# K pages of the paged cache kept in natural layout, turned in place in 32x32 blocks by VectorE and scored in 32-row, 32-column tiles of TensorE, 16 pages at a time

## Chip, cores and metric

One core of one Trainium2 chip runs the whole program once. The metric is the device time in microseconds. The kernel before took 1212.95 us (median of 3 runs, 1209.15 to 1214.07).

## What is computed

One layer of a hybrid decoder, for one prompt of 512 positions and for 8 samples of 8 new positions each, with the same weights. The part that the change touches is the attention of the samples to their paged cache: 32 pages of 128 keys per sample, 8 heads of 64.

```python
def sb_logits(q, k, sb_bias):
    z = jnp.einsum("bqhd,bkhd->bhqk", q, k).astype(jnp.float32) * SB_SCALE
    return z + sb_bias.astype(jnp.float32)[None, :, None, None]

def sb_block(z, mask, v, carry):
    log_om = jnp.where(mask, jax.nn.log_sigmoid(-z), 0.0)
    suffix = lax.cumsum(log_om, axis=3, reverse=True) - log_om + carry[..., None]
    a = jnp.where(mask, jnp.exp(jax.nn.log_sigmoid(z) + suffix), 0.0)
    o = jnp.einsum("bhqk,bkhd->bqhd", a, v.astype(jnp.float32))
    return o, carry + jnp.sum(log_om, axis=3)

    def page_step(state, phys):
        o_acc, carry = state
        kp = cache_k[phys]
        vp = cache_v[phys]
        zp = sb_logits(q, kp, sb_bias)
        o_p, carry = sb_block(zp, True, vp, carry)
        return (o_acc + o_p, carry), None
```

The pages of a sample are taken from the newest to the oldest, since each needs the product of the (1 - beta) of all newer keys. The rest of the layer is: the input projection (q, k, v and three convolution inputs), the same attention inside the prompt, a gated convolution, the output projection, cross attention to a memory of 256 tokens, and a SwiGLU of width 2816. All is float32. The large products are made of three passes over a high and a low part of each operand (`w_hi`, `w_lo`, `h_hi`, `h_lo`).

## The kernel before

Five in-order instruction streams (TensorE, VectorE, ScalarE, GpSimd, SyncE) are written out by hand and meet at semaphores. The program has a front of 32 **chunks** and, behind them, the output projection, cross attention and the SwiGLU. The samples are worked on in 4 groups of two; a group has 8 chunks, and a chunk has 4 pages of each of the two samples, 8 pages of 256 KB for K and as many for V. SyncE issues the K pages (`k_pages`, L610) and the weights, GpSimd issues the V pages (`v_pages`, L610) and makes the low parts of weights (`tile_lo`, L940).

What chunk C does, in the order of TensorE's stream (`group`, which calls the functions named here):

- `k_transposes(C + 1)` (L1651): 8 pages, 4 transposes of 128x128 each, through three PSUM banks. ScalarE copies the even pages out (`copy_k`, L1029) and VectorE the odd ones (`copy_k`, L1307), to `kT`, where the 64 dimensions of two heads lie on the 128 partitions.
- `tile(2C + 2)` (L1570): 128 columns of the input projection, in chunks 0 to 10; VectorE scales the result out of PSUM (`evac`, L1291, L1295). Of the 32 tiles, 24 belong to the prompt and sample projection and 8 to the memory (`mem_tile_chunk`).
- `weight_transposes` (L1687) for chunk C, then `prompt_transposes` (L1623) of an earlier unit of prompt attention.
- `scores(C + 1)` (L1676): 8 matmuls of 128 rows and 32 columns against 512 keys, four column tiles side by side.
- `tile(2C + 3)`, again in chunks 0 to 10; `prompt_scores(u)` (L1611, L1614), where u = C - LAST counts 16 units of prompt attention (4 head pairs by 4 query blocks, the number of key blocks is u mod 4 plus 1).
- `sums(C)` (L1708): the weights of 8 pages times V; `prompt_sums` (L1636).

ScalarE makes the two sigmoids of a chunk's scores (`sample_sigmoids`, L1035 and L1037) and of the prompt's (`prompt_sigmoids`, L1057), and copies weights out of PSUM. VectorE makes the suffix products with a scan and multiplies (`weights`, L1317, L1324, L1327 for the samples; `prompt_weights`, L1334, L1340 for the prompt), and copies half of the prompt's transposed weights (`copy_prompt_weights`, L1348). In VectorE's stream a chunk is: `evac`, `copy_k`, `evac`, in some chunks a piece of the convolution, `copy_prompt_weights`, `prompt_weights`, `weights`. At a group's end it copies the sums out (L1414), TensorE transposes them, and VectorE copies the result into place (L1419). `queries` (L1354) lays the next group's queries block-diagonally into `q_bd`.

The waits that set the order around the change are these lines. A page's slot is free when it has been transposed:

```python
if C:
    sp.wait_ge(s_ktr, 8 * C + q - 7)
```

and the scores of a chunk wait for both copying engines:

```python
pe.wait_ge(m_["k_copied_a"], 4 * C + 4)
pe.wait_ge(m_["k_copied_d"], 4 * C + 4)
```

V pages have 10 slots in the chunks before LAST and 12 after it.

## Time and profile before

| | before |
|---|---|
| runs | 1212.95 us median (1209.15 to 1214.07) |
| profiled execution, own time | 1204.37 us |
| its span, first to last instruction | 1202.7 us |
| granted TensorE clock, mean | 0.978 |
| TensorE busy | 1107.7 us (92%) |
| VectorE busy | 624.4 us (52%) |
| ScalarE busy | 397.0 us (33%) |
| GpSimd busy | 409.1 us (34%) |
| read from HBM | 213.78 MB |
| chain that ended last: TensorE, VectorE, DMA | 75%, 12%, 7% |

The busy shares are averages over stretches with different limits. The front ends at about 595 us; what follows is almost all dense matmul. A float32 matmul that is not split into high and low parts shows as two records in the trace, one per pass; a transpose shows as one. Where matmuls run side by side in tiles of the array, the busy time of a group is the time in which at least one of them ran, and its mean is that of one record, from start to drained end.

### The profile page before, as it was taken

The page shows a single profiled execution, that of the slowest core. Times are in us where ns is not written, and L with a number is a line of the kernel's source. Part 1 is how long each engine was busy: PE and PEld are TensorE (multiplying, and loading weights), DVE is VectorE, ACT ScalarE, POOL GpSimd, SP SyncE. Part 2 cuts the span into 40 slices and gives each one's busy share as a digit, 9 for nine tenths or more (in the row PEclk, how much of TensorE's full clock was granted, in tenths as well). Part 3 has the DMA queues.
Part 4 walks back from the last instruction along what each step waited for, and adds up shares of the span by engine and source line. Part 5 has one row for each costly group of instructions (what it writes and reads, how often), then busy time and mean ns, then how long its engine had stood idle before and what let it go on. Part 6 is the DMA issues. An engine that isn't in the chain of part 4 may idle for free.

```text
span 1202.7 us, 25986 instructions
## 1 busy us (share of the span) xinstructions
PE 1107.7 (92%) x9831; PEld 978.0 (81%) x9831; DVE 624.4 (52%) x854; ACT 397.0 (33%) x624; POOL 409.1 (34%) x341
## 2 busy tenths in 40 slices
PE   6799999899697999899699888899999999999997
PEld 3687888777465777667599858899999999999996
DVE  2645535644555776675588357655543002544544
ACT  3533323233453655453523162412111112112121
POOL 0425344432322443344342003333433333433330
PEclk9899999999988999999899999899999999999999
DMA  9858676855997889897752033222221223231212
GB/s 348 303 153 303 226 289 217 281 203 189 373 333 271 302 316 353 318 363 275 238 210 70 29 112 106 71 82 93 70 87 53 92 88 100 70 105 44 66 65 78
DMA packets 126489, 220.96 MB, mean 184 GB/s; under 512 B 9951, under 2 KB 68580, under 8 KB 126388
## 3 DMA queue, kind: packets, MB, share of 16 engines
q1 hardware_dynamic: 103234, 146.63, 35.5%
q0 software_dynamic: 20480, 67.13, 15.7%
q10 hardware_dynamic: 2674, 5.87, 1.4%
q8 instruction: 62, 1.02, 0.3%
q14 instruction: 39, 0.32, 0.1%
HBM read 213.78 MB, written 5.80 MB: 183 GB/s over the span
## 4 chain that ended last, share of the span: by engine, by line
PE 75%; DVE 12%; DMA 7%; issue 2%; ACT 2%; SPq 2%; POOLq 0%; POOL 0%; DVEq 0%; ACTq 0%
PE ps L513 38%; PE ps L1570 14%; PE ps L1651 8%; PE ps L1676 4%; DMA k_page<-in_cache_sb_k 3%; PE ps L1708 3%; PE ps L574 2%; DMA mw_raw<-in_w_in 2%; DVE r_sq L671 1%; DVE h_lo L418 1%; DVE r_sum L676 1%; DVE run L1334 1%; DMA v_late<-in_cache_sb_v 1%; DVE run_s L1317 1%; DVE aw L1340 1%
## 5 line engine op out<-in xcount | busy, mean ns | idle before, releaser
L469 POOL TENSOR_TENSOR w_lo<-w_raw,w_hi 128x2048 fp32r<-128x2048 f32 (+3 forms) x49 | 192.9, 3939 | 395.4 <-ACT w_hi L446 359.7
L513 PE MATMUL ps<-h_hi,w_hi 128*128 128x288 f32 x832 | 180.0, 298 | 8.7 <-DVE h_lo L418 5.7
L513 PE MATMUL ps<-h_lo,w_hi 128*128 128x288 f32 x832 | 179.2, 297 | 0.0
L513 PE MATMUL ps<-h_hi,w_lo 128*128 128x288 f32 x832 | 179.1, 297 | 0.0
L1651 PE MATMUL ps<-cc,k_page 128*128 128x128 f32 x1024 | 142.0, 290 | 36.5 <-DVE kT L1307 14.2
L1651 PEld LDWEIGHTS ps<-cc,k_page 128*128 128x128 f32 x1024 | 117.8, 148 | 59.5 <-issue 44.2
L446 ACT ACTIVATE w_hi<-w_raw 128x2048 fp32r<-128x2048 f32 (+3 forms) x47 | 77.9, 1660 | 255.1 <-PE ps L513 227.2
L610 POOL DMA_DIRECT2D v_late<-in_cache_sb_v x168 | 90.3, 537 | 171.5 <-issue 109.4
L513 PEld LDWEIGHTS ps<-h_hi,w_hi 128*128 128x128 f32 x832 | 135.2, 190 | 9.8 <-issue 7.2
L513 PEld LDWEIGHTS ps<-h_hi,w_lo 128*128 128x128 f32 x832 | 135.1, 190 | 0.0
L513 PEld LDWEIGHTS ps<-h_lo,w_hi 128*128 128x128 f32 x832 | 135.1, 190 | 0.0
L1307 DVE COPY kT<-ps 128x512 f32<-128x512 f32 x128 | 87.8, 691 | 90.4 <-PE ps L1651 90.1
L940 POOL TENSOR_TENSOR mw_lo<-mw_raw,mw_hi 128x1024 fp32r<-128x1024 f32 x32 | 78.9, 2466 | 109.3 <-ACT mw_hi L1010 109.2
L1029 ACT ACTIVATE kT<-ps 128x512 f32<-128x512 f32 x128 | 75.9, 597 | 105.4 <-PE ps L1651 105.1
L1570 PE MATMUL ps<-h_hi,mw_hi 128*128 128x288 f32 (+1 forms) x288 | 81.0, 336 | 2.9 <-DVE h_lo L418 2.8
L1570 PE MATMUL ps<-h_hi,mw_lo 128*128 128x288 f32 (+1 forms) x288 | 78.7, 328 | 0.0
L1570 PE MATMUL ps<-h_lo,mw_hi 128*128 128x288 f32 (+1 forms) x288 | 78.4, 327 | 0.0
L610 POOL DMA_DIRECT2D v_early<-in_cache_sb_v x88 | 47.6, 542 | 88.9 <-PE ps L1708 53.9
L513 PE MATMUL ps<-f_hi,w_hi 128*128 128x288 f32 x352 | 75.4, 296 | 0.0
L513 PE MATMUL ps<-f_lo,w_hi 128*128 128x288 f32 x352 | 75.4, 296 | 0.0
L513 PE MATMUL ps<-f_hi,w_lo 128*128 128x288 f32 x352 | 75.3, 296 | 0.0
L666 DVE TENSOR_TENSOR xT<-ps,xT 128x576 f32<-128x576 f32 (+1 forms) x32 | 24.2, 758 | 97.8 <-PE ps L513 97.2
(252 smaller groups left out, 1818.9 us busy)
## 6 DMA issues: line engine op xcount, KB each, us to landing
k_page<-in_cache_sb_k SPq DMA_DIRECT2D x256, 256.0 KB, 5.2
v_late<-in_cache_sb_v POOLq DMA_DIRECT2D x168, 256.0 KB, 5.2
v_early<-in_cache_sb_v POOLq DMA_DIRECT2D x88, 256.0 KB, 4.9
mw_raw<-in_w_in SPq DMA_DIRECT2D x12, 1024.0 KB, 5.2
w_raw<-in_w_gate SPq DMA_DIRECT2D x11, 1024.0 KB, 5.3
w_raw<-in_w_up SPq DMA_DIRECT2D x11, 1024.0 KB, 5.4
w_raw<-in_w_down SPq DMA_DIRECT2D x8, 768.0 KB, 4.2
w_raw<-in_w_down SPq DMA_DIRECT2D x8, 640.0 KB, 4.0
```

The source lines that it names most:

```text
L446: nc.scalar.activation(w_hi[s][:, 0:KN[name], :], w_raw[s][:, 0:KN[name], :], ACT.Copy).then_inc(s_whi, 1)
L469: return nc.gpsimd.tensor_tensor(w_lo[s][:, ks, :], w_raw[s][:, ks, :], w_hi[s][:, ks, :].bitcast(F32), ALU.subtract)
L513: op = nc.tensor.matmul(ps[:, 2 * t + hf, 0:b - a], weights[s][:, k, t * P:(t + 1) * P], x[:, k0 + k, a:b], start=begin and k == ks[0] and ...
L610: eng.dma_start(slot, cache[0, bass.ds(page, 1)].rearrange("o p h d -> p o (h d)")).then_inc(loaded, 16)
L666: nc.vector.tensor_tensor(x, pair(j % 2), x, ALU.add).then_inc(s_free[name], 1)
L940: nc.gpsimd.tensor_tensor(mw_lo[j // 2 % 2][:, :, t], mw_raw[j // 2 % 2][:, :, t], mw_hi[j % 2][:, :, :].bitcast(F32), ALU.subtract).then_ ...
L1029: nc.scalar.activation(kT[:, q // 4, :, (q % 4) * P:(q % 4 + 1) * P], tiled(ps[:, q % 3, :]), ACT.Copy).then_inc(m_["k_copied_a"], 1)
L1307: nc.vector.tensor_copy(kT[:, q // 4, :, (q % 4) * P:(q % 4 + 1) * P], tiled(ps[:, q % 3, :]))\
L1570: op = nc.tensor.matmul(ps[:, bank, 0:b - a], weights, x[:, k, a:b], start=k == 0 and w == 0, stop=k == KD - 1 and w == 2)
L1651: op = nc.tensor.transpose(ps[:, q % 3, j * P:(j + 1) * P], k_page[:, q, j * P:(j + 1) * P], ident)
L1676: op = nc.tensor.matmul(ps[32 * j:32 * j + 32, 3, :], q_bd[:, s, j, :], kT[:, s, j, :], start=s == 0, stop=s == 1)
L1708: op = nc.tensor.matmul(ps[32 * j:32 * j + 32, 6, s * P:(s + 1) * P], awT_s[C >= LAST][:, q, 32 * j:32 * j + 32], page[:, 0, j * P:(j + 1) ...
```

## The change

The four functions of the K path are replaced. Pages are loaded in **halves**: half H = 2U + s is 8 pages of one of the group's two samples (s), and the pair of halves U is 16 pages, as much as two chunks. There are two sets of 8 page slots (`k_set`), one per sample; SyncE may fill a set when the scores of the half that lay in it are made. VectorE turns two pages at a time in place, in 32x32 blocks (`k_blocks`, one instruction of 128x1024, four to a half). After that, partition group `a` (32 partitions) holds 32 dimensions of the keys 32a to 32a + 31, and TensorE scores a half with 64 matmuls of 32 rows, 32 columns and 256 keys (`half_scores`): 2 halves of the dimensions, 4 head pairs, 4 row groups that write PSUM banks 0 to 3, and 2 heads that take two of the four column groups. The queries are spread for this by `query_blocks` on TensorE (16 small matmuls a group) and by 24 small copies on VectorE in `queries`.

The sigmoids, scans and products are made for a pair of halves, at odd chunks: one sigmoid of 1024 columns (beta), and twice a sigmoid of 512 (1 - beta), a scan, a product and a copy of the carry (`page_sigmoids`, `page_weights`, parts 0 and 1). `om_s` is now scanned in place, so that the second sigmoid waits for the first scan and carry. At the head of an even chunk TensorE waits until the second sigmoid has read the score banks (`banks_read`), since its memory tiles and items use banks 1 to 3. The new positions' scores have rows of their own (`new_scores`, `new_sigmoids`, `new_weights`), at the seventh chunk of a group.

`sums` keeps its columns but takes 2 matmuls of 256 columns a page in place of 4 of 128; the closing matmuls with `zeros` are gone. Prompt attention begins at chunk 12 in place of 11, V pages have 8 and then 10 slots, and the tiles of the memory go in pairs in chunks 18, 20, 26 and 28. GpSimd's order within a chunk is low part, 4 pages, low part, 4 pages.

```diff
-LAST = 11
-V1, V2 = 10, 12
+LAST = 12
+V1, V2 = 8, 10
...
+        q_new = at("q_new", [2 * P], R_P + T_B * T * 4 + 8192)
+        q_blk = [at(f"q_blk{i}", [8 * P], off) for i, off in enumerate((R_W + 40960, R_H + 20480))]
+        beta_s = at("beta_s", [2 * SEQ], R_V + 10240)
...
-        k_page = at("k_page", [8, CH], R_M)
+        k_set = [at(f"k_set{s}", [8, CH], off) for s, off in enumerate((R_M, R_W + 16384))]
...
-        kT = at("kT", [2, HP, SEQ], R_W + 16384)
...
-        def k_pages(sp, C):
-
+        def k_half(sp, H):
+
+            U, s = divmod(H, 2)
+            if H >= 2:
+                sp.wait_ge(m_["half"], H - 1)
             for q in range(8):
-                if C:
-                    sp.wait_ge(s_ktr, 8 * C + q - 7)
-                load_page(sp, C, q, ck, k_page[:, q:q + 1, :], s_kp[q // 2])
+                load_page(sp, 64 * (U // 4) + 32 * s + 24 - 8 * (U % 4) + q, ck, k_set[s][:, q:q + 1, :], s_kp[s][q // 4])
...
-            def copy_k(C):
-
-                for q in range(0, 8, 2):
-                    if q == 0 and C:
-                        act.wait_ge(m_["score"], 9 * ((C - 1) // 8) + (C - 1) % 8 + 2)
-                    act.wait_ge(s_ktr, 8 * C + q + 1)
-                    nc.scalar.activation(kT[:, q // 4, :, (q % 4) * P:(q % 4 + 1) * P], tiled(ps[:, q % 3, :]),
-                                         ACT.Copy).then_inc(m_["k_copied_a"], 1)
-
-            def sample_sigmoids(S, w):
-                act.wait_ge(m_["score"], S + 1)
-                act.wait_ge(m_["weight"], S)
-                nc.scalar.activation(beta_s[:, 0:w], ps[:, 3, 0:w], ACT.Sigmoid, scale=SB_SCALE,
-                                     bias=bias_s[:, 0:1])
-                nc.scalar.activation(om_s[:, 0:w], ps[:, 3, 0:w], ACT.Sigmoid, scale=-SB_SCALE,
-                                     bias=bias_s[:, 1:2]).then_inc(m_["om"], 1)
...
+
+            def page_sigmoids(U, part):
+
+                S = 9 * (U // 4) + 2 * (U % 4) + 1 + part
+                if part == 0:
+                    act.wait_ge(m_["half"], 2 * U + 2)
+                    nc.scalar.activation(beta_s[:, :].rearrange("p (g a k) -> p g a k", a=4, k=32),
+                                         ps[:, 0:4, 0:256].rearrange("p a (g k) -> p g a k", k=32), ACT.Sigmoid,
+                                         scale=SB_SCALE, bias=bias_s[:, 0:1])
+                c0 = P * (1 - part)
+                act.wait_ge(m_["run"], 2 * S)
+                nc.scalar.activation(om_s[:, 0:SEQ].rearrange("p (g a k) -> p g a k", a=4, k=32),
+                                     ps[:, 0:4, c0:c0 + P].rearrange("p a (g k) -> p g a k", k=32), ACT.Sigmoid,
+                                     scale=-SB_SCALE, bias=bias_s[:, 1:2]).then_inc(m_["om"], 1)
...
+            def k_blocks(H, ns):
+
+                U, s = divmod(H, 2)
+                for n in ns:
+                    dve.wait_ge(s_kp[s][n // 2], 64 * (U + 1))
+                    pages = k_set[s][:, 2 * n:2 * n + 2, :].rearrange("p a f -> p (a f)")
+                    nc.vector.transpose(pages, pages).then_inc(s_kt, 1)
...
+            def page_weights(U, part):
+
+                S = 9 * (U // 4) + 2 * (U % 4) + 1 + part
+                dve.wait_ge(m_["om"], S + 1)
+                om_ = om_s[:, 0:SEQ][:, ::-1]
+                nc.vector.tensor_tensor_scan(om_, om_, om_, om_s[:, SEQ:SEQ + 1], ALU.mult, ALU.bypass)\
+                    .then_inc(m_["run"], 1)
+                dve.wait_ge(m_["run"], 2 * S + 1)
+                b = beta_s[:, SEQ * (1 - part):SEQ * (2 - part)]
+                nc.vector.tensor_tensor(b, b, om_s[:, 1:SEQ + 1], ALU.mult).then_inc(m_["weight"], 1)
                 dve.wait_ge(m_["weight"], S + 1)
-                nc.vector.tensor_copy(run_s[:, SEQ:SEQ + 1], run_s[:, 0:1]).then_inc(m_["run"], 1)
-                dve.wait_ge(m_["run"], R + 2)
+                nc.vector.tensor_copy(om_s[:, SEQ:SEQ + 1], om_s[:, 0:1]).then_inc(m_["run"], 1)
+                dve.wait_ge(m_["run"], 2 * S + 2)
...
+                bank = 4 if G == 0 else 0
+                dve.wait_ge(m_["spread"], G + 1)
                 for s in range(2):
                     for h2 in range(2):
-                        op = nc.vector.tensor_copy(
-                            q_bd[64 * h2:64 * h2 + 64, s, :, 16 * s + 8 * h2:16 * s + 8 * h2 + 8],
-                            pT[64 * h2:64 * h2 + 64, T_Q:T_Q + HP, SEQ + 16 * G + 8 * s:SEQ + 16 * G + 8 * s + 8])
+                        for e in range(2):
+                            q = ps[:, bank, (2 * h2 + e) * NS:(2 * h2 + e + 1) * NS].rearrange("p (j s t) -> p j s t", s=2, t=TS)
+                            n = (4 * s + 2 * h2 + e) * P
+                            first, last = diagonal(q_blk[G // 2][:, n:n + P])
+                            nc.vector.tensor_copy(first, q[:, 0:3, s, :])
+                            nc.vector.tensor_copy(last, q[:, 3, s, :])
...
                 op.then_inc(m_["queries"], 1)
...
-                    if 2 * C + 1 < TILES:
+                    if C and 2 * C + 1 < TILES:
                         evac(2 * C + 1)
-                    if C + 1 < CHUNKS:
-                        copy_k(C + 1)
-                    if C == 0:
-                        weights(1, 3, SEQ)
-                    if c == 7 and not last:
+                    if c == 6 and not last:
                         queries(g + 1)
+                    for j in MEM_TILES.get(C, ()):
+                        evac(j)
+                    if C + 2 < CHUNKS:
+                        k_blocks(C + 2, range(2, 4) if C else range(4))
                     if 2 * C + 2 < TILES:
...
+                    if c % 2 and C + 1 < CHUNKS:
+                        page_weights(C // 2 + 1, 0)
+                    if c == 6 and not last:
+                        new_weights(g + 1)
                     if 1 <= u < 17:
                         prompt_weights(u - 1)
-                    if c < 7:
-                        weights(9 * g + c + 2, 19 * g + 5 + 2 * c, SEQ)
+                    if c % 2 and C + 1 < CHUNKS:
+                        page_weights(C // 2 + 1, 1)
                     if C == LAST + 5:
                         lo_parts(dve, "ck", mT, G_MEM, range(KD))
-                if not last:
-                    weights(9 * g + 9, 19 * g + 19, NS)
-                else:
+                    if C + 3 < CHUNKS:
+                        k_blocks(C + 3, range(2))
...
+            def banks_read(C):
+
+                pe.wait_ge(m_["om"], 9 * (C // 8) + C % 8 + 3)
...
+            def half_scores(H):
+
+                U, s = divmod(H, 2)
+                pe.wait_ge(s_kt, 4 * H + 4)
+                pe.wait_ge(m_["queries"], U // 4 + 1)
+                blk = q_blk[U // 8]
+                for e in range(2):
                     for j in range(HP):
...
+                        for a in range(4):
+                            for h2 in range(2):
+                                r, c, n = slice(32 * a, 32 * a + 32), 32 * (2 * s + h2), (4 * s + 2 * h2 + e) * P + 32 * j
+                                d = (2 * j + h2) * HD + 32 * e
+                                op = nc.tensor.matmul(tiled(ps[c:c + 32, a, 0:2 * P], 32), blk[r, n:n + 32],
+                                                      k_set[s][r, :, d:d + 32], start=e == 0 and j == 0,
+                                                      stop=e == 1 and j == HP - 1)
+                op.then_inc(m_["half"], 1)
...
                     C, u = 8 * g + c, 8 * g + c - LAST
-                    if C + 1 < CHUNKS:
-                        k_transposes(C + 1)
-                    if C == LAST - 1:
-                        scores_read(C)
-                        early_banks(C + 1)
-                        rms_pe(pe, "conv", c_sq[:, 0, :], T, None, 2)
+                    if c % 2 == 0:
+                        banks_read(C)
+                    if c == 6 and not last:
+                        query_blocks(g + 1)
+                    if C == 10:
+                        rms_pe(pe, "conv", c_sq[:, 0, :], T, None, 0)
+                    items(C)
+                    for j in MEM_TILES.get(C, ()):
+                        tile(j)
                     if 2 * C + 2 < TILES:
                         tile(2 * C + 2)
-                    if C in ITEMS:
-                        scores_read(C)
-                        early_banks(min(C + 1, CHUNKS - 1))
-                        items(C)
-                    if mem_tile_chunk(C):
-                        scores_read(C)
-                        tile(mem_tile_chunk(C))
                     weight_transposes(9 * g + c + 1, 4, u - 2)
                     if 2 <= u < 18:
                         prompt_transposes(u - 2)
-                    if C == LAST - 1:
+                    if C == 10:
                         pe.wait_ge(s_rt["conv"], 1)
-                    if c < 7:
-                        scores(C + 1)
-                    elif not last:
-                        new_scores(g + 1)
+                    if C in ITEMS:
+                        pe.wait_ge(s_ic, FIRST_ITEM[C + 1])
+                    if C in MEM_TILES:
+                        pe.wait_ge(s_gf, MEM_TILES[C][1] + 1)
+                    if C + 2 < CHUNKS:
+                        half_scores(C + 2)
                     if 2 * C + 3 < TILES:
                         tile(2 * C + 3)
                     if 0 <= u < 16:
                         prompt_scores(u)
+                    if c == 6 and not last:
+                        new_scores(g + 1)
                     sums(C)
                     if 2 <= u < 18:
+                        if c == 6 and not last:
+                            pe.wait_ge(m_["om"], 9 * g + 10)
```

VectorE's stream before, chunk 20, inside prompt attention (`mkT` is a tile of the memory, `awT` the prompt's transposed weights, `run` and `aw` the two heads of a unit, the last three rows the samples):

```order
L1307 COPY kT<-ps 128x4x128 x4
L1297 TENSOR_TENSOR mkT<-ps,rstd_m 128x256
L1348 COPY awT<-ps 128x512
L1334 SCALAR_TENSOR_TENSOR run<-om 128x128
L1340 TENSOR_TENSOR aw<-beta,run 128x128
L1334 SCALAR_TENSOR_TENSOR run<-om 128x128
L1340 TENSOR_TENSOR aw<-beta,run 128x128
L1317 SCALAR_TENSOR_TENSOR run_s<-om_s,run_s 128x512
L1324 TENSOR_TENSOR beta_s<-beta_s,run_s 128x512
L1327 COPY run_s<-run_s 128x1
```

VectorE's stream now, the odd chunk 17, with the same unit types (two of the first row's turns end chunk 16's part; `k_set_111` and `k_set_112` are the two sets):

```order
L1314 STREAM_TRANSPOSE k_set_112<-k_set_112 128x1024 x4
L1360 COPY awT<-ps 128x512
L1333 SCALAR_TENSOR_TENSOR om_s<-om_s 128x512
L1337 TENSOR_TENSOR beta_s<-beta_s,om_s 128x512
L1339 COPY om_s<-om_s 128x1
L1346 SCALAR_TENSOR_TENSOR run<-om 128x128
L1352 TENSOR_TENSOR aw<-beta,run 128x128
L1346 SCALAR_TENSOR_TENSOR run<-om 128x128
L1352 TENSOR_TENSOR aw<-beta,run 128x128
L1333 SCALAR_TENSOR_TENSOR om_s<-om_s 128x512
L1337 TENSOR_TENSOR beta_s<-beta_s,om_s 128x512
L1339 COPY om_s<-om_s 128x1
```

The copies out of PSUM became turns in SBUF; the samples' weights moved in front of the prompt's and again behind them, in odd chunks alone. Every chunk has four turns, two at its head and two at its end.

TensorE's stream before, chunk 16 (`cc,aw` are the prompt's transposes, L1611 and L1614 its scores):

```order
L1651 MATMUL ps<-cc,k_page 128x128 x32
L1687 MATMUL ps<-cc,beta_s 128x128 x4
L1623 MATMUL ps<-cc,aw 128x128 x8
L1676 MATMUL ps<-kT,q_bd 32x512 x8
L1611 MATMUL ps<-pT 128x256 x2
L1614 MATMUL ps<-cc 128x128 x2
L1708 MATMUL ps<-v_late,awT_s_106 32x128 x32
L1636 MATMUL ps<-awT,v_tok 64x128 x8
```

and now, chunk 17, with the same unit of prompt attention:

```order
L1724 MATMUL ps<-cc,beta_s 128x128 x4
L1649 MATMUL ps<-cc,aw 128x128 x8
L1708 MATMUL ps<-k_set_112,q_blk_104 32x256 x64
L1637 MATMUL ps<-pT 128x256 x2
L1640 MATMUL ps<-cc 128x128 x2
L1750 MATMUL ps<-v_late,awT_s_107 32x256 x16
L1662 MATMUL ps<-awT,v_tok 64x128 x8
```

The transposes at the head are gone, and the scores, behind the same two groups of small transposes, became 64 matmuls.

## Rows read from the trace of the kernel before

**Rows 1.** Windows of the front, core 0 (columns in the first line)

```profile
core 0: us, PE busy (x) PEld busy (x) DVE busy (x) ACT busy (x) POOL busy (x), PEclk, DMA share, GB/s
69.60:288.40 218.80, 212.95 (x1950) 176.07 (x1948) 106.65 (x166) 68.48 (x98) 89.52 (x98) 0.99 0.68 239
288.40:304.60 16.20, 15.79 (x159) 12.11 (x158) 7.92 (x10) 6.38 (x12) 3.35 (x7) 1.00 0.61 202
304.60:537.00 232.40, 203.92 (x2422) 152.00 (x2422) 145.57 (x233) 119.53 (x234) 84.33 (x139) 0.96 0.92 328
537.00:595.00 58.00, 48.18 (x629) 38.52 (x629) 29.02 (x39) 26.39 (x42) 26.44 (x33) 0.93 0.80 275
```

**Rows 2.** Chain of work, one chunk of the tile stretch (start us, us, what)

```profile
96.72 1.85 PE ps L1676 x16
98.57 5.69 PE ps L1570 x24
104.26 1.89 PE ps L1708 x64
106.14 4.03 PE ps L1651 x32
110.17 6.39 PE ps L1570 x48
```

**Rows 3.** Groups by form, whole run (count, busy us, mean ns, idle before, releasers)

```profile
L1651 PE MATMUL ps<-cc,k_page 128*128 128x128 f32 x1024 | 142.0, 290 | 36.5 <-DVE kT L1307 14.2 <-DMA k_page<-in_cache_sb_k 8.5 <-ACT kT L1029 6.8
L1317 DVE TENSOR_TENSOR_SCAN run_s<-om_s,run_s 128x512 f32<-128x512 f32 x32 | 44.9, 1403 | 39.1 <-ACT om_s L1037 39.1
L1324 DVE TENSOR_TENSOR beta_s<-beta_s,run_s 128x512 f32<-128x512 f32 x32 | 24.6, 768 | 1.1
L1035 ACT ACTIVATE beta_s<-ps,bias_s 128x512 f32<-128x512 f32 x32 | 22.0, 688 | 28.8 <-PE ps L1676 28.8
L1291 DVE TENSOR_TENSOR pT<-ps,rstd 128x288 f32<-128x288 f32 x24 | 9.9, 452 | 34.6 <-PE ps L1570 34.5
L1676 PEld LDWEIGHTS ps<-kT,q_bd 128*32 128x32 f32 x512 | 13.8, 109 | 26.2 <-issue 24.3 <-ACT k_rows L1021 0.9 <-ACT v_tok L1021 0.6
```

**Rows 4.** Timeline of TensorE, three places (start us, us, engine, what)

```profile
96.65 1.92 PE L1676 MATMUL ps<-kT,q_bd 128*32 128x512 f32 x16
...
710.19 1.93 PE L827 MATMUL ps<-smkT,qc 128*32 128x256 f32 x32
...
472.41 1.13 PE L1611 MATMUL ps<-pT 64*128 64x512 f32 x4
```

**Rows 5.** Groups by form, operations on VectorE like the added ones

```profile
L1354 DVE COPY q_bd<-pT 64x32 f32<-64x32 f32 x16 | 2.9, 182 | 0.2
L1348 DVE COPY awT<-ps 128x512 f32<-128x512 f32 x4 | 2.8, 692 | 3.1 <-PE ps L1623 3.1
L1265 DVE TENSOR_SCALAR pT<-pT,cvec 128x576 f32<-128x576 f32 x4 | 2.1, 520 | 0.1
L1348 DVE COPY awT<-ps 128x256 f32<-128x256 f32 x4 | 1.7, 425 | 2.9 <-PE ps L1623 2.9
```

**Rows 6.** Groups of 290 to 595 us, VectorE and ScalarE in prompt attention

```profile
L1334 DVE TENSOR_TENSOR_SCAN run<-om 128x128 f32<-128x128 f32 (+3 forms) x32 | 28.3, 884 | 0.1
L1340 DVE TENSOR_TENSOR aw<-beta,run 128x128 f32<-128x128 f32 (+3 forms) x32 | 25.7, 804 | 1.1
...
L1057 ACT ACTIVATE beta<-ps,bias_p 128x128 f32<-128x128 f32 (+3 forms) x32 | 16.9, 528 | 11.5 <-DVE aw L1340 9.1 <-PE ps L1614 2.4
...
L1348 DVE COPY awT<-ps 128x128 f32<-128x128 f32 (+3 forms) x16 | 7.9, 492 | 10.3 <-PE ps L1623 10.3
...
L418 DVE SCALAR_TENSOR_TENSOR m_lo<-mT,cvec,m_hi 128x256 fp32r<-128x256 f32 x8 | 3.3, 480 | 0.0
```

**Rows 7.** Chain of work, prompt attention (start us, us, what)

```profile
411.26 2.87 PE ps L1570 x24
...
431.40 2.67 DVE aw L1340
```

More of the change, by code:

```diff
@@ L950, in _ @@
             v_pages(pool, 0, range(8))
-            v_pages(pool, 1, range(2))
             tile_lo(2)
@@ L1807, in shape_table @@
     c[i, C_ID + i] = 1.0
[L1808 removed]
+    seq, step_ = i // 64, i % 8
     for g in range(GROUPS):
```

306 lines of the change are left out of this document (146 added, 160 removed).

## Prediction

> **What bounds the kernel now.** I read the windows first. The front is three different stretches, and behind 595 us nothing is changed. From 69.6 to 288.4 us (chunks 0 to 10, the tile stretch) TensorE is busy 212.95 of 218.80 us at a DMA share of 0.68: TensorE bounds it. From 304.6 to 537.0 us (chunks 12 to 27, prompt attention) TensorE is busy 203.92 of 232.40, VectorE 145.57, and the DMA share is 0.92 at 328 GB/s: three resources are near their ends at once. The rest, 16.20 and 58.00 us, is between the two [rows 1]. Second, the chain of waits: in the tile stretch it is TensorE alone, where a chunk is scores 1.85, a tile of 5.69, sums 1.89, transposes 4.03, a tile of 6.39 [rows 2]. In prompt attention it changes between TensorE and VectorE's prompt weights, one product of which took 2.67 us [rows 7]. Third, the groups give the price of each operation.
>
> The sum is made on the profiled execution, 1204.37 us; the median is 1212.95, a factor of 1.0071, which I apply at the end.
>
> **What goes from TensorE.** Per chunk 4.03 us of transposes and 1.85 us of scores [rows 2]. With them go the copies to `kT` and TensorE's waits for them (14.2 on VectorE, 6.8 on ScalarE, 8.5 on K pages, whole run [rows 3]). The K pages' DMAs stay the same in number; they are now issued when a half's scores are made, two chunks ahead of use, so I take their 8.5 us as gone.
>
> **The 64 small matmuls.** Each has two passes of 256 columns. The nearest rows: 16 records of 512 columns in four column tiles take 1.92 us, 32 records of 256 columns in four column tiles 1.93 us. So four tiles side by side pass 256 columns in 1.93 / 8 = 0.24, or 0.22 without the ends. Two row groups also run side by side: four records of 512 columns over 64 rows take 1.13 us [rows 4], where four in a row would need about 4 x 0.43. From this I take that all eight tiles (four row groups, two column groups) run together: 128 records / 8 = 16 passes x 0.216 + 0.13 for the drain = 3.6 us. The bounds are 3.6 (eight together) and 32 x 0.216 = 6.9 (four together); I take the low end since both kinds of sharing have a row. Per chunk TensorE gets -4.03 - 1.85 + 3.6 = **-2.3 us**.
>
> The rows show weight loads of 109 ns hidden under matmuls of other column tiles on the same rows: 16 loads lie in the 1.92 us [rows 3, 4]. The Trainium skill, "TensorE: Matmul & The Clock Gate", Part 3 (Packing small matmuls), says that a load overlaps matmuls in flight only when its row group differs. By that rule the two column groups of a row group would stand in each other's way; what this gives is rival H.
>
> **The turn.** No row shows a transpose on VectorE. A multiply by a scalar, SBUF to SBUF, does 576 columns in 0.520 us, so 1024 would take 0.92: the lower bound. A scan does 512 in 1.40 [rows 3, 5], so 1024 would take 2.6 by its column rate less a fixed part: the upper bound. A plain copy does 256 in 0.425 and 512 in 0.692 [rows 5], 1.04 ns a column, so 1024 take 1.2 us. A turn moves every element once as a copy does: I take 1.2. The Trainium skill, "Vector Engine (DVE) Microarchitecture Reference", section 3.8, says that a 32x32 transpose keeps one element per cycle and lane; with the 0.96 GHz of its page "VectorE: DVE Perf Modes" that is an estimate of 1.07 us, by which the sum below would be 10 us lower. No run here shows it.
>
> **Tile stretch.** TensorE's 11 chunks get 11 x -2.3 = -25. But the pair's weights now hang in one chain behind the odd chunk's half, and the next chunk's tile needs the tile before it out of its bank, for which VectorE's evacuation stands behind all of them in its stream: beta 1024 columns 1.1, 1 - beta 0.7, scan 1.4, product 0.8, carry 0.15, 1 - beta 0.7, scan 1.4, product 0.8, carry 0.15, two turns 2.4, evacuation 2 x 0.45, handovers 0.5 (durations of [rows 3], the sigmoid of 512 is 0.69) = 11.0 us. Cover on TensorE is a tile (mean of 5.69 and 6.39, 6.04) and sums 1.89 = 8 [rows 2]. 3.0 us are bare in each of five odd chunks: +15. Net **-10**. The group's boundary and the start (0 to 69.6) I take as they are.
>
> **Prompt stretch.** VectorE's stream for a pair of chunks, busy time: 8 turns 9.6; prompt weights of two units, 4 x (0.884 + 0.804) = 6.75; two copies of 0.49 [rows 6]; page weights 2 x (1.30 + 0.77 + 0.15) = 4.4 (the scan is a little shorter here than its 1.40 over the run). Sum 21.8. What it waits for inside the loop: the odd chunk's half, whose turns stand right ahead in its own stream, 3.6 less the 0.5 of the copy = 3.1; then ScalarE's beta of 1024 columns and 1 - beta, 1.8; then, between the scans, the sigmoids of the second head, 2 x 0.53 [rows 6], and the second 1 - beta, together 1.7; eight handovers of 0.1. Together **29.2 us a pair**. That is longer than the DMA's pair, 2 x 4.19 MB (16 pages of 256 KB) at 328 GB/s [rows 1] = 25.6, and than TensorE's, which was 204 / 8 = 25.5 and loses 4.6. So VectorE's loop sets 8 pairs: 234 us. Outside it:
> - two group boundaries, 13.7 each: 24 small copies of 0.182 [rows 5] = 4.4; the wait for the new positions' scores, queued behind the half and prompt scores on TensorE (3.6 + 1 + 0.8, and a sigmoid 0.6) = 6.0; their weights 0.9; closing copies 0.42 + 0.5 + 8 x 0.19 = 2.4. Sum 27.
> - tiles of the memory in pairs in four chunks: 2 x 2.87 [rows 7] and an evacuation 0.85, over some 4.7 us of VectorE's own work, 2 each: 8.
> - the memory's low parts, 8 x 0.48 [rows 6]: 4.
>
> 234 + 27 + 8 + 4 = 273 against 232.4: **+41**. In the kernel before, the copies of K pages overlapped TensorE's transposes of the same chunk; now turns, the scores that need them, and the weights that need those follow each other on one engine.
>
> V pages: with 8 slots, later 10, six of a chunk's eight wait for the sums of the chunk before, and their transfer of some 12 us is just covered by a chunk of 14.6: nothing. The other queues get no longer.
>
> **The remaining chunks** (11, 12, 29 to 31, now without the K transposes) go at the DMA's pace, 5 x 12.8 + 5 = 69 against 16.2 + 58.0 [rows 1]: **-5**.
>
> Sum: -10 + 41 - 5 = +26, so 1204.4 + 26 = 1230, and x 1.0071 = **1239 us**.
>
> **Rivals.**
> - **F, faster (0.23).** Transfers, not VectorE, set the prompt's chunks. The DMA share of 0.92 speaks for it, and my waits inside the loop (7.4 of 29.2) are worked out, not seen; if ScalarE and TensorE run ahead of them, the loop is under 25.6. Then tiles -25 + 5, prompt 16 x 12.8 + 20 = 225 (-7), rest -5: -32, 1172, or 1181 on the median's scale. With every chunk at the DMA's pace and no extras, -51: 1162.
> - **S, no change (0.12).** The loop is shorter by 2.5 to 4 us a pair than I took: 8 of them take back the 26. About 1213.
> - **H, the halves are slower (0.10).** The tiles do not run eight together, so the change doesn't do what it says. If the second column group's load is not hidden, 16 x (0.216 + 0.110) = 5.2, +1.6 in 11 + 8 places = +31: 1261, or 1270. With four tiles together, +3.3 x 19 = +62: 1292, or 1301. Against it speak the rows with loads hidden on the same rows.
> - **T, turns at the scan's rate (0.07).** 2.6 us each: +1.4 x 64 turns in the prompt stretch = +90, and +14 in the five stalls: 1334, or 1343. From 1.5 us a turn on VectorE sets everything. Against it: a turn has no chain from one element to the next.
>
> **The numbers.** My own case has 0.48 and a range of 1219 to 1270. Its rival of the other sign is F. About 0.5% (1207 to 1219) is what a measurement of this kernel can tell from no change; S fills it. Faster 0.23 (F), same 0.12 (S), slower 0.48 + 0.10 + 0.07 = 0.65. The range takes in F but its best part, and H up to four tiles together, and leaves out T: 1165 to 1300.
>
> **What would show it.** Right: in the windows of prompt attention VectorE busy over 0.7 and DMA share at or under 0.85; pairs of chunks about 29 us apart; turns of 1.2 us; 128 records of half scores in 3.6 us; in odd chunks of the tile stretch a wait of about 3 us of TensorE's tile for VectorE's evacuation. Wrong: pairs of 26 us with a DMA share over 0.9 (F), halves of 5 us or more (H), turns of 2 us or more (T), a front that ends before 595 us less 10.

## Result and profile after

The changed kernel takes 1281.19 us (median of 4 runs, 1276.16 to 1285.54) against 1211.74 us for the kernel before (median of 4 runs beside it): 1.057 times as long, 95% interval 1.052 to 1.063, so 69.5 us slower. The forecast was slower by 26 us, 1239, in a range up to 1300. The sign was right and the time lies in the range; the size is not: the change costs 2.7 times what was worked out.

The profiled execution of the changed kernel took 1285.54 us, a little over its median, and that of the kernel before 1204.37, a little under its own. The two spans differ by 81.2 us where the medians differ by 69.5; what follows divides the 81.2.

Windows of both kernels, cut at the same points of the program: the starts of the first matmuls of `sums(0)` and `sums(10)`; of the sums of the first chunk with prompt attention (11 before, 12 after) and of those 16 chunks later; and the first operation of the output projection. Columns as in [rows 1]. Before:

```profile
0.00:84.80 84.80, 64.50 (x454) 49.65 (x454) 35.78 (x63) 35.73 (x63) 19.28 (x19) 0.96 0.76 269
84.80:296.00 211.20, 205.35 (x1878) 167.50 (x1879) 102.95 (x160) 67.32 (x96) 87.14 (x97) 0.99 0.70 247
296.00:307.50 11.50, 11.09 (x141) 8.46 (x140) 8.21 (x8) 5.86 (x11) 4.84 (x9) 1.00 0.72 245
307.50:538.80 231.30, 202.82 (x2419) 151.34 (x2422) 144.34 (x233) 119.71 (x234) 82.98 (x137) 0.96 0.92 328
538.80:595.70 56.90, 47.08 (x619) 38.65 (x612) 28.04 (x43) 24.90 (x40) 26.57 (x33) 0.92 0.79 268
595.70:1202.70 607.00, 576.82 (x4337) 562.38 (x4335) 305.12 (x351) 143.49 (x182) 188.27 (x47) 0.99 0.26 86
```

After:

```profile
0.00:97.80 97.80, 69.12 (x790) 53.36 (x790) 51.01 (x89) 31.25 (x54) 17.51 (x17) 0.90 0.75 260
97.80:315.10 217.30, 192.40 (x2397) 152.40 (x2397) 119.99 (x182) 42.75 (x51) 88.79 (x100) 0.95 0.73 237
315.10:345.90 30.80, 20.47 (x353) 12.53 (x352) 24.57 (x24) 5.96 (x9) 9.65 (x18) 0.79 0.97 335
345.90:638.40 292.50, 208.83 (x3336) 143.67 (x3336) 178.59 (x277) 82.95 (x165) 87.02 (x136) 0.82 0.74 258
638.40:672.90 34.50, 23.93 (x333) 14.77 (x327) 12.83 (x25) 12.46 (x20) 16.46 (x24) 0.82 0.64 195
672.90:1283.90 611.00, 580.47 (x4334) 565.20 (x4332) 305.03 (x351) 143.49 (x182) 188.13 (x47) 0.98 0.26 85
```

Line by line: start +13.0; tile stretch +6.1; the 16 chunks of prompt attention +61.2; the chunks beside them 65.3 against 68.4, -3.1; everything behind the front +4.0. In prompt attention TensorE is busy in 71% of the time (88% before), VectorE in 61% (62% before), the DMA share is 0.74 (0.92 before). Nothing is nearly full, where before TensorE and the DMA queues were, and the granted clock is 0.82 where it was 0.96. That points at the order in which the engines wait for each other; the experiments test it.

The added operations (groups by form):

```profile
L1314 DVE STREAM_TRANSPOSE k_set<-k_set 128x1024 f32<-128x1024 f32 x128 | 150.3, 1219 | 5.3 <-DMA k_set<-in_cache_sb_k 4.0
L1708 PE MATMUL ps<-k_set,q_blk 32*32 32x256 f32 x4096 | 132.6, 409 | 25.9 <-DVE k_set L1314 14.4 <-issue 11.5
L1037 ACT ACTIVATE beta_s<-ps,bias_s 128x1024 f32<-128x1024 f32 x16 | 17.8, 1110 | 41.7 <-PE ps L1708 41.7
L1333 DVE TENSOR_TENSOR_SCAN om_s<-om_s 128x512 f32<-128x512 f32 x32 | 55.5, 1735 | 98.2 <-ACT om_s L1042 98.1
```

A turn takes 1.2 us (median 1.203), as taken. What VectorE and TensorE wait for between 345 and 638 us (the waits view: engine, line, releaser: us in total, times, longest; the largest rows of each):

```profile
DVE om_s L1333 <- ACT om_s L1042: 64.0, 16, 10.6
DVE om_n L1321 <- ACT om_n L1029: 16.0, 2, 8.2
DVE awT L1360 <- PE ps L1649: 15.5, 7, 3.9
DVE mkT L1303 <- PE ps L1600: 8.2, 4, 2.8
DVE pT L1303 <- PE ps L1600: 5.5, 3, 2.5
PE ps L1792 <- DVE o_pair L1440: 19.9, 2, 10.1
PE ps L1750 <- DMA v_late<-in_cache_sb_v: 19.3, 11, 2.7
PE ps L1708 <- DVE k_set L1314: 11.9, 4, 4.8
```

VectorE is idle 114 of the 292.5 us. The forecast had about 71 of it: 53 for the scores' sigmoids, 12 for the new positions', 6 for handovers. What it had not at all is the third row: VectorE waits for TensorE's transposes of the prompt weights, which stand in TensorE's stream behind the chunk before.

TensorE's two largest waits are not in the forecast either. At each of the two group ends it waits 10 us for VectorE to copy the sums out (L1440), which stands in VectorE's stream behind the second page weights and two turns; before, this wait was 1.3 us in all. And it waits 19.3 us for V pages, where the forecast said "nothing" and the kernel before waited 3.7 (between 307.5 and 538.8 us). The chain that ended last passes through a V page only once in this stretch (at 576.64, for 6.63 us), so most of these waits run beside it.

The chain of one pair with memory tiles (start us, us, what), the changed kernel:

```profile
423.14 3.70 PE ps L1708 x128
...
426.87 1.11 ACT beta_s L1037
427.98 0.59 ACT om_s L1042
...
428.59 3.60 DVE om_s L1333
...
433.97 0.47 ACT beta L1063
434.44 0.36 ACT om L1065
...
435.53 0.59 ACT om_s L1042
...
436.14 1.30 DVE om_s L1333
...
438.38 3.27 DVE m_lo L416 x8
...
441.78 7.75 PE ps L1600 x48
...
450.19 2.39 issue
452.58 5.34 PE ps L1708 x128
```

From one odd half to the next (463 us) it is 40 us. The chain goes once round TensorE, ScalarE and VectorE: half, sigmoids, scan (3.60 here, where the second one takes 1.30; see the last section), the prompt's sigmoids that stand in ScalarE's stream ahead of the second 1 - beta, the second scan, low parts, two memory tiles, two turns that stand in VectorE's stream behind those tiles (the 2.39), the next half. And TensorE's two entries are slow: a half takes 3.7 us when the engine was busy before, 5.34 here; the 48 tile records 7.75, where two such tiles took 2 x 2.87 before [rows 7].

### The profile page after: what moved, and what is told of

It is laid out like the page before. It is cut to its first block, busy times and chain, and to the rows that moved or that the text cites. A ratio compares the mean times of both kernels' runs of the same rounds, so it can differ in the third digit from the quotient of the medians.

```text
span 1283.9 us, 29001 instructions
## 1 busy us (share of the span) xinstructions
PE 1095.2 (85%) x11527; PEld 941.9 (73%) x11527; DVE 692.0 (54%) x945; ACT 318.9 (25%) x480; POOL 407.6 (32%) x341
## 4 chain that ended last, share of the span: by engine, by line
PE 62%; DVE 18%; DMA 7%; ACT 5%; issue 4%; SPq 2%; POOLq 1%; POOL 0%; DVEq 0%; ACTq 0%
PE ps L511 35%; PE ps L1600 8%; PE ps L1708 8%; DMA mw_raw<-in_w_in 5%; DVE om_s L1333 3%; DVE k_set L1314 3%; PE ps L572 2%; PE ps L1750 2%; DVE r_sq L673 1%; DVE beta_s L1337 1%; ACT om_s L1042 1%; DVE r_sum L678 1%; DVE h_lo L416 1%; DMA v_late<-in_cache_sb_v 1%; SPq L606 1%
## 5 line engine op out<-in xcount | busy, mean ns | idle before, releaser
L607 POOL DMA_DIRECT2D v_late<-in_cache_sb_v x160 | 85.8, 537 | 235.7 <-PE ps L1750 157.8
L1708 PE MATMUL ps<-k_set,q_blk 32*32 32x256 f32 x4096 | 132.6, 409 | 25.9 <-DVE k_set L1314 14.4
L1314 DVE STREAM_TRANSPOSE k_set<-k_set 128x1024 f32<-128x1024 f32 x128 | 150.3, 1219 | 5.3 <-DMA k_set<-in_cache_sb_k 4.0
L1708 PEld LDWEIGHTS ps<-k_set,q_blk 32*32 32x32 f32 x4096 | 85.8, 113 | 63.7 <-issue 32.8
L1600 PE MATMUL ps<-h_hi,mw_hi 128*128 128x288 f32 (+1 forms) x288 | 86.8, 358 | 30.0 <-DVE pT L1301 13.5
L1333 DVE TENSOR_TENSOR_SCAN om_s<-om_s 128x512 f32<-128x512 f32 x32 | 55.5, 1735 | 98.2 <-ACT om_s L1042 98.1
L1600 PEld LDWEIGHTS ps<-h_hi,mw_hi 128*128 128x128 f32 x288 | 53.4, 207 | 43.7 <-issue 31.4
L1600 PE MATMUL ps<-h_lo,mw_hi 128*128 128x288 f32 (+1 forms) x288 | 83.4, 346 | 0.0
L1600 PE MATMUL ps<-h_hi,mw_lo 128*128 128x288 f32 (+1 forms) x288 | 83.2, 345 | 0.0
L607 POOL DMA_DIRECT2D v_early<-in_cache_sb_v x96 | 51.9, 542 | 98.4 <-PE ps L1750 70.3
```

The lines of the kernel that those rows point to most:

```text
L607: eng.dma_start(slot, cache[0, bass.ds(page, 1)].rearrange("o p h d -> p o (h d)")).then_inc(loaded, 16)
L1314: nc.vector.transpose(pages, pages).then_inc(s_kt, 1)
L1333: nc.vector.tensor_tensor_scan(om_, om_, om_, om_s[:, SEQ:SEQ + 1], ALU.mult, ALU.bypass)\
L1600: op = nc.tensor.matmul(ps[:, bank, 0:b - a], weights, x[:, k, a:b], start=k == 0 and w == 0, stop=k == KD - 1 and w == 2)
L1708: op = nc.tensor.matmul(tiled(ps[c:c + 32, a, 0:2 * P], 32), blk[r, n:n + 32], k_set[s][r, :, d:d + 32], start=e == 0 and j == 0, stop=e = ...
```

## Experiments

Each is compared with the kernel before, run on the same chip; where two experiments are compared they can come from different chips, on which the kernel before had medians of 1212 to 1214 us. Theory C: a chain over the engines sets the time, and TensorE's clock falls in the gaps. Theory D: pages and weights arrive late.

**e1: turns of 32 columns.**

```diff
-                    nc.vector.transpose(pages, pages).then_inc(s_kt, 1)
+                    nc.vector.transpose(pages[:, 0:32], pages[:, 0:32]).then_inc(s_kt, 1)
```

> The changed kernel, but each turn on VectorE covers 32 of its 1024 columns (pages stay almost unturned, so the scores are wrong numbers); all waits stay. Changed kernel 1281 us, kernel before 1212. Theory C (a chain of halves, sigmoids, page weights, turns and the next half leaves TensorE idle, and its clock falls): four of a pair's turns lie in the chain, 4.4 us in 8 pairs and 2.2 in five stalls, about -46, and some -15 from a better clock: 1220. Theory D (V pages and weights arrive late): at most -10, about 1272.

1220.87 us, ratio 1.010 (1.006 to 1.015). The pages stay almost unturned here, so the scores are wrong numbers; only the time counts. The turns are worth 60 us in this order, of 132 us that they now spare VectorE. But without them the kernel is still 1% slower than the one before: a second cause is needed.

**e2: filler at the head of even chunks.**

```diff
                     if c % 2 == 0:
+                        if C and 0 <= C < 32:
+                            if u - 2 > 0:
+                                pe.wait_ge(p_["out_copied"], min(u - 2, 4 * GROUPS))
+                            pe.wait_ge(m_["tr_copied"], 9 * g + c + 1)
+                            for _ in range(8):
+                                nc.tensor.matmul(ps[:, 4, 0:SEQ], ident, cc[:, 0:SEQ], start=True, stop=True)
                         banks_read(C)
```

> The changed kernel with 8 filler matmuls of 512 columns (3.5 us at full clock) into a free bank at the head of every even chunk, where TensorE waits for the second sigmoid. Theory C: the halves of prompt attention go from about 5.4 back to 3.7 us and the tiles of the memory from 7.8 to 5.8, worth 15 to 25 us: 1260. If the lost clock is only a companion of waits that are set elsewhere: 1281 or a little more.

1350.75 us, ratio 1.113 (1.108 to 1.118): 70 us slower than the changed kernel. Two things went wrong with the test. The filler was twice as long as meant: it took 7.13 us in the seven chunks where the granted clock was 1.00, and 9.0 to 9.8 us in the other eight, at 0.73 to 0.79. And it needed a free bank, and the copy that frees it stands in ScalarE's stream behind the very sigmoid that TensorE waits for; in chunks 18, 20 and 28 the filler began only after a wait of 3.5 to 5.9 us and added its whole length. Timeline of e2 in chunk 18:

```profile
468.64 9.29 PE L1763 MATMUL ps<-cc 128*128 128x512 f32 x16 [5.85 <-ACT pT L1078]
```

The time therefore says nothing on what the clock costs. The rows behind the filler say a little: all four pairs of memory tiles took 6.3 us there, where they take 6.9 to 8.1 in the changed kernel, and of the four halves behind them two took 3.69 us and two still 5.1 and 5.3. Together that is some 7 us, bought with 34 us of filler in these four chunks.

**e8: filler without a wait.**

```diff
                         prompt_sums(u - 2)
+                    if c in (1, 3, 5) and 12 < C < 28:
+                        for _ in range(12):
+                            for r in range(0, P, 32):
+                                nc.tensor.matmul(ps[r:r + 32, 6, 0:2 * P], cc[64:P, C_CMASK:C_CMASK + 32],
+                                                 cc[64:P, 0:2 * P], start=False, stop=False)
```

> The changed kernel with filler matmuls that add zeros to the sums (12 x 4 of 32 columns against 256, some 5.2 us at full clock) at the end of chunks 13, 17, 19, 21, 25 and 27, with no wait of their own, so inside TensorE's idle time. Theory C: the tiles of the memory in chunks 18, 20, 26 and 28 take 5.8 instead of 7.8 us and the halves behind them 3.7 instead of 5.4: up to -14, 1267. If the clock is no part of the loss: 1281 or more.

1315.06 us, ratio 1.084 (1.079 to 1.089). Windows and chain of e8 at chunk 25:

```profile
590.00:600.00 10.00, 8.00 (x76) 4.43 (x80) 8.12 (x12) 2.31 (x6) 5.69 (x10) 0.67 0.93 333
600.00:610.00 10.00, 10.00 (x72) 6.88 (x64) 0.59 (x1) 0.00 (x0) 0.54 (x1) 0.50 0.36 134
```

```profile
594.73 10.40 PE ps L1793 x96
605.13 8.32 PE ps L1600 x48
```

Here the filler ran at a granted 0.50, took 10.4 us in place of 5.2, and pushed the memory tiles back. So it was in four of its six places (10.47 us each, start to drained end); in the other two, chunks 17 and 21, it ran at 1.00 and took 5.38. Behind the one at chunk 17 the two memory tiles took 5.98 us in place of 7.75, but the half behind them still 5.12. Theory C's gain in time did not show, and the test failed as a test: this filler cost more than it gave. How much of the time is the clock's own is left to the rows below.

**e3: weights issued ahead of K pages** (two blocks of SyncE's stream exchanged).

```diff
-                if C + 2 < CHUNKS:
-                    k_half(sp, C + 2)
                 if 2 <= C + 1 < TILES // 2 or C + 1 in (13, 14):
                     load_tiles(C + 1 if C < 12 else C)
+                if C + 2 < CHUNKS:
+                    k_half(sp, C + 2)
```

> The changed kernel, SyncE issues a slot of projection weights ahead of the next half's eight K pages instead of behind them. Theory D: weights now land in 5 instead of 10 us, ScalarE is not held up ahead of the sigmoids, and the five stalls of the tile stretch shrink by 2 to 3 us: 1268. Theory C: the stall is VectorE's evacuation behind two page weights and two turns, at most -5: 1277.

1269.82 us, ratio 1.050 (1.045 to 1.054): 11 us back. The weights' median time to landing went from 10.1 to 5.2 us. It is theory D's number, and it comes from the tile stretch (217.3 to 206.6 us), but not from five stalls alike: from half 11 to half 13 it is 6.6 us less (39.1 to 32.5), in each of the five pairs ahead 0.1 to 2.7.

**e4: the kernel before with 8 and 10 V slots.**

```diff
-V1, V2 = 10, 12
+V1, V2 = 8, 10
```

(GpSimd's order in a chunk goes with it: low part, 4 pages, low part, 4 pages.)

> The kernel before with the changed kernel's V slots (8 and 10) and GpSimd's order; nothing else. Theory D: fewer slots cost 15 to 25 us here as well: about 1232. Theory C: 1212 to 1218.

1214.60 us, ratio 1.0016 (0.9994 to 1.0039). In the kernel before the slots alone cost nothing that can be measured. Of the changed kernel this says less: there TensorE waits 19.3 us for V pages inside prompt attention, here 5.5. No run gives the changed kernel more slots, so that part of theory D is open.

**e5: ScalarE's second 1 - beta ahead of the prompt's sigmoids.**

```diff
+                    if c % 2 and C + 1 < CHUNKS:
+                        page_sigmoids(C // 2 + 1, 1)
                     if 0 <= u < 16:
                         prompt_sigmoids(u)
-                    if c % 2 and C + 1 < CHUNKS:
-                        page_sigmoids(C // 2 + 1, 1)
```

> The changed kernel (1281 us), ScalarE makes the second 1 - beta ahead of the prompt's four sigmoids instead of behind them. Theory C: this sigmoid, and with it the second scan, the turns behind it and TensorE's next chunk come 1.5 to 2 us earlier in each of 8 pairs: 1267. If VectorE's work alone sets the pace (it has the prompt's weights to do in between anyway): 1281.

1261.87 us, ratio 1.040 (1.035 to 1.045): 19 us back, 2.4 a pair on average; prompt attention alone is 23 us shorter (292.5 to 269.5).

**e6: three places in the order of VectorE and TensorE.**

```diff
-                    if C and 2 * C + 1 < TILES:
+                    if C and c % 2 and 2 * C + 1 < TILES:
                         evac(2 * C + 1)
+                    if C + 2 < CHUNKS:
+                        k_blocks(C + 2, range(2, 4) if C else range(4))
                     if c == 6 and not last:
                         queries(g + 1)
                     for j in MEM_TILES.get(C, ()):
                         evac(j)
-                    if C + 2 < CHUNKS:
-                        k_blocks(C + 2, range(2, 4) if C else range(4))
...
+                    if c % 2 and 2 * C + 3 < TILES:
+                        evac(2 * C + 3)
                     if c % 2 and C + 1 < CHUNKS:
                         page_weights(C // 2 + 1, 1)
...
+                    early = C in ITEMS or C in MEM_TILES or C == 10 or (c == 6 and not last)
-                    if c % 2 == 0:
+                    if c % 2 == 0 and early:
                         banks_read(C)
```

(where it is not early, `banks_read` stands ahead of `half_scores`.)

> The changed kernel with three moves in the written order: VectorE turns pages ahead of query copies and memory tiles; evacuates tile 2C+3 of an odd chunk between the two page weights; TensorE waits for the score banks at the half, not at the chunk's head, where nothing uses them. Theory C: tiles no longer wait behind page weights and turns (3 to 4 us in five places), halves behind memory tiles no longer wait for a turn (2.4 us in four): 1281 - 17 - 10 = 1254. If the waits are the weights' arrival or V pages: 1275 to 1281.

1247.78 us, ratio 1.028 (1.023 to 1.033): 33 us back. The pairs from half 3 to 7 went from 42.6 and 44.2 to 36.4 and 37.5 us, near 2 x 18.0. (In the kernel before it is 20.3 us from scores to scores; less the forecast's 2.3 that gives 18.0 of TensorE's own work.) The tile stretch is 19.7 us shorter, prompt attention 16.3.

**e7: e3, e5 and e6 together.**

> e3, e5 and e6 together. Theory C with D's queue part: 1281 - 11 - 14 - 25 = 1231; still over the kernel before, since the chain from half to half over three engines remains.

1224.19 us, ratio 1.009 (1.0065 to 1.012). Of 69.5 us, 57 are gone without one instruction less. The three parts add up to 64 alone, so they overlap by 7 us only.

**e10: e7 with turns of 32 columns.**

> e7 with turns of 32 of 1024 columns (pages almost unturned, scores wrong numbers). What the turns cost in the better order, and what is left without them. Theory C: like in e1, 35 to 45 us less than e7: 1185. If something else has taken over (transfers at 25.6 us a pair): 1195.

1195.40 us, ratio 0.985 (0.983 to 0.987). In this order the turns are worth 29 us, and what is left, with its wrong scores, is 1.5% under the kernel before. It is the second number of the expectation, but that transfers have taken over is not shown: the DMA share is 0.87 between 297 and 557 us, and TensorE waits 24.0 us for V pages there.

**e9: e7 with four turns in VectorE's idle time.**

```diff
+                    if c % 2 and C + 3 < CHUNKS:
+                        k_blocks(C + 3, range(4))
                     if c % 2 and C + 1 < CHUNKS:
                         page_weights(C // 2 + 1, 0)
```

(The turns at the head of even chunks and at the end of odd ones go in return.)

> e7 (1224 us), and VectorE makes all four turns of the next even half inside the odd chunk, ahead of the page weights, where it waits some 4.7 us for the scores' sigmoids; until now they stood behind the second page weights and in the next chunk. Theory C: four turns, 4.8 us, leave the chain of 8 pairs of prompt attention less some 1.5 for what spills over, and 2 us each the tile stretch's pairs: 1224 - 26 - 8 = 1190, and under the kernel before. If K pages are not there by then or VectorE's total work binds: 1224 or above.

1257.66 us, ratio 1.037 (1.035 to 1.039): 33 us slower than e7. VectorE's timeline in one odd chunk:

```profile
412.06 2.37 DVE L1314 STREAM_TRANSPOSE k_set<-k_set 128x1024 f32<-128x1024 f32 x2 [2.13 <-DMA k_set<-in_cache_sb_k]
418.35 2.37 DVE L1314 STREAM_TRANSPOSE k_set<-k_set 128x1024 f32<-128x1024 f32 x2 [3.92 <-DMA k_set<-in_cache_sb_k]
```

The half that frees the set ended at 403.3; SyncE then issues eight pages at 1.09 us each, and the last landed at 418.3, 15 us later. VectorE waited 71.6 us for K pages in the whole run, in e7 7.9. With one set per sample all four turns can't be this early: in e7 the transfers had been hidden behind the page weights.

**e11: e9 with the memory's low parts a chunk earlier.**

> e9, and the memory's high and low parts are made a chunk earlier (at the end of chunk 16 in place of 17), where VectorE is not in the chain. Theory C: the 3.3 us in front of the first memory tile go: 3 us less than e9. If they only move: the same as e9.

1250.72 us, ratio 1.030 (1.028 to 1.032): 7 us less than e9, twice what was expected; where the rest comes from was not looked into.

**e12: e7 with two turns early, evacuations ahead of turns.**

```diff
+                    if c % 2 and C + 3 < CHUNKS:
+                        k_blocks(C + 3, range(2))
                     if c % 2 and C + 1 < CHUNKS:
                         page_weights(C // 2 + 1, 0)
+                    if c % 2 == 0 and 2 * C + 3 < TILES:
+                        evac(2 * C + 3)
...
-                    if C + 3 < CHUNKS:
+                    if c % 2 == 0 and C + 3 < CHUNKS:
                         k_blocks(C + 3, range(2))
```

(The evacuation of tile 2C + 1 at the chunk's head goes in return.)

> e7 (1224 us), and of the next even half only the two turns whose pages land first stand ahead of the first page weights; the other two stay where they were; each tile's evacuation comes ahead of the turns in every chunk. Reading of e9: there K pages 4 to 7 landed 15 us after the set came free and VectorE waited 72 us for them. Theory C: two turns leave the chain of each pair without that wait: 8 x 2.4 and some 10 in the tile stretch, 1224 - 25 = 1199. If K pages of the first two turns are late too: 1215 to 1224.

1211.74 us, ratio 0.998 (0.9956 to 1.0006), half of the gain expected: no difference from the kernel before. The wait for K pages is 24.4 us in the run, not 7.9.

**e13: e12 with the low parts a chunk earlier; e14: e12 with turns of 32 columns.**

> e12 with the memory's high and low parts a chunk earlier, as in e11. Theory C: 3 to 6 us less than e12. If they only move: the same.

> e12 (1212 us) with turns of 32 of 1024 columns (pages almost unturned, scores wrong numbers). If two of a pair's four turns in the chain are now covered, the turns cost less here than in e7 (where 1.09 us less a turn gave 29 us): some 15, 1197. If their place made no difference: 29 again, 1183.

e13: 1209.31 us, ratio 0.997 (0.994 to 0.999), an interval that overlaps with e12's; its own gain is not shown. e14, again with wrong scores: 1194.22 us, ratio 0.984 (0.982 to 0.986). Without turns both orders end at the same time (1195.4 and 1194.2); with them e12 is 12 us better. So nearly all of e12's gain is covered turns: they are worth 60 us in the changed kernel, 29 in e7, 17.5 in e12.

By stretch, in the profiled executions (us; start up to `sums(0)`, tile stretch to `sums(10)`, the 16 chunks of prompt attention):

| | start | tile stretch | prompt attention |
|---|---|---|---|
| kernel before | 84.8 | 211.2 | 231.3 |
| changed kernel | 97.8 | 217.3 | 292.5 |
| e7 | 96.9 | 195.4 | 258.3 |
| e12 | 98.6 | 191.4 | 244.0 |
| e14, turns of 32 columns | 92.8 | 188.3 | 239.2 |

With the order mended, TensorE's gain in the tile stretch is there, 20 us of the 25 forecast. The start stays 12 to 14 us longer, and prompt attention 13 us longer in e12, 8 without the turns. So the change breaks even, and no order tried here makes it faster.

## Why the prediction was right on the sign and wrong on the size

- **Durations: right.** The turn was taken at 1.2 us; its rows have a median of 1.203. The 1.07 that was estimated from the Trainium skill ("Vector Engine (DVE) Microarchitecture Reference", section 3.8) is 11% low. A half was taken at 3.6 us and takes 3.68, with eight tiles side by side, four of which share rows with the other four. So rival H is out, and with it, for this pattern of loads, the rule of the Trainium skill, "TensorE: Matmul & The Clock Gate", Part 3, that a load overlaps matmuls in flight only when its row group differs.
- **Tile stretch: forecast -10, measured +6.** The gain of TensorE is there: from an even half to the odd one it is 18.2 us in the first two pairs after the start, where 20.3 less 2.3 gives 18.0. TensorE's waits there for VectorE's evacuations sum to 18 us, where 15 were taken (waits between 76 and 305 us):

```profile
PE ps L1600 <- DVE pT L1301: 13.5, 3, 4.8
PE ps L1600 <- DVE vT L1301: 2.5, 1, 2.5
PE ps L1600 <- DVE pT L1297: 2.1, 1, 2.1
```

  A step that failed here is "the other queues get no longer": the projection weights land in 10.1 us, in the kernel before in 5.6, and e3, which mends this, takes 10.7 us from the stretch. The clock is in it too: behind a stall a tile of 48 records takes 8.0 us in place of 6.4. What the group's boundary, taken as unchanged, adds was not measured apart.
- **Start: forecast 0, measured +13.** It was passed over ("I take as they are"). Two halves, twelve turns and the first pair's page weights now stand between VectorE's first tile evacuations: the first starts 4.6 us later than before (53.9 and 49.3 us), the third 11.2 (87.3 and 76.1). No order tried takes this back.
- **Prompt stretch: forecast +41, measured +61.** The step that failed is "VectorE's loop sets 8 pairs", 29.2 us each: from odd half to odd half it is 32 to 40 us, 36.6 a pair with everything. Of the signs named, pairs of about 29 us and VectorE busy over 0.7 did not come (0.61). VectorE's busy time was not too low: 178.6 us, where 8 x 21.8 and the extras give some 197. But a sum over one engine's stream supposes that this engine waits only in the places that one has listed. In these 292.5 us the chain that ended last is on TensorE for 150, on VectorE for 88 and on ScalarE for 28. The real loop leaves VectorE in every pair, and e5 and e6 found the places: a sigmoid behind the prompt's four (counted, 1.7 us, but as unavoidable), turns behind memory tiles that they don't need, a bank wait at a chunk's head where nothing uses the bank. Together, in e7, they take 34 us from this stretch, more than the 20 by which the forecast was short.
- **Terms that the sum did not have.** At each group end TensorE waits 10 us for the copy of the sums; the sum had the copies as VectorE's time only. And the page scan was taken at 1.30 us, but four of the 16 in this stretch took 3.6 to 4.7, 12 us more together, because GpSimd's low parts of the memory tiles ran beside them; three of the four lie in the chain. Neither was taken away by itself in a run. The reading "three resources are near their ends at once" had also put VectorE too high: 145.57 of 232.40 us is 63%.
- **The clock: taken as no term, it is one.** Of the 16 halves between 346 and 638 us eight took 5.0 to 6.1 us and not 3.7, 14.1 us together; the memory tiles took 6.9 to 8.1 us a pair in place of the 5.98 that a pair took at full clock in e8, 6.6 together. These 21 us are rows of TensorE at its lower level behind gaps, and lie mostly in the chain. They are not all: the granted clock was at 0.50 for 107 of the 292.5 us (before for 17 of 231.3), and TensorE was busy 208.8 us where 204 less 8 x 4.6 gives 167. Since clock, scans and group ends sum to more than the 20 us by which this term was short, other terms of the sum were too high. That the 21 us would vanish with the gaps, e7 and e12 bear out only in part (the slow halves in that stretch fall from eight to four and two, while the order changes too); the two filler tests did not separate it.
- **Rival F** (transfers set the pace) was wrong: the DMA share fell to 0.74. **Rival T** was wrong: a turn takes 1.2 us. **Rival S** was wrong: the loop is longer, not shorter. What none of them named is that most of the loss is order: 57 of 69.5 us.

## What to carry to other kernels

When an operation moves to another engine, its duration is the easy part; write down for each engine what stands behind the moved step in its stream, and walk the loop once round over all engines, with the clock that TensorE has after each gap and with what GpSimd does beside each scan. Before judging such a change, try the orders of the same instructions: here they were worth 70 us, from 5.7% slower to no difference. A buffer that is refilled only after its last use sets a floor under how early the next step can go (15 us here), and an earlier place in the stream then blocks the engine.

## What was not expected of the hardware

- The scan of 512 columns takes 1.28 us alone and 3.58 us beside a GpSimd product. Timeline of VectorE and GpSimd, changed kernel:

```profile
428.59 3.58 DVE L1333 TENSOR_TENSOR_SCAN om_s<-om_s 128x512 f32<-128x512 f32 x1 [4.72 <-ACT om_s L1042]
```

```profile
426.41 4.67 POOL L943 TENSOR_TENSOR mw_lo<-mw_raw,mw_hi 128x1024 fp32r<-128x1024 f32 x2
```

  The scan ends 1.1 us after GpSimd's second product does. So do the other three long ones: at 468.56 it takes 4.72 us, beside GpSimd's 467.50 to 472.18. Of the 32 page scans of the changed kernel the eight that started while such a product ran took 1.87 to 4.71 us; one, at 77.97, beside which a product only started, took 1.28. In the kernel before the same shows in a product of 2.67 us on VectorE, from 431.40 on, beside GpSimd's 431.14 to 433.52 [rows 7]; the scan's mean of 1.40 in [rows 3] has seven such cases in it, of 1.65 to 2.01 us.
- A turn of 32 columns takes 0.17 us, one of 1024 1.20: 0.14 fixed and 1.04 ns a column, that of a plain copy from PSUM.
- In e8 the granted clock was 0.50 from 593.4 to 610.5 us, although TensorE was busy without a gap from 592.0 us on, from 594.7 with filler of 64 rows and 32 columns and from 605.1 with memory tiles of 128 by 128. From 610.5 to 617.3 us it was 1.00.
